# Turning the context, the raw tokens and the spatial weights in small pieces between the first weight chunks of a two-block transformer kernel

## What is computed

```python
def first_block(x, norm1_g, w_in, v_norm_g, w_s, b_s, ...):
    h = rmsnorm(x, norm1_g[l])
    proj = h @ w_in[l]
    u, v_a, q, k, v_b = jnp.split(proj, splits, axis=-1)
    y_a = chunked_spatial_gating(u, v_a, v_norm_g[l], w_s[l], b_s[l])
    q = rmsnorm(q.reshape(bsz, s, B_HEADS, 2, B_HEAD_DIM), q_norm_g[l]).transpose(0, 2, 3, 1, 4)
    k = rmsnorm(k.reshape(bsz, s, B_HEADS, 2, B_HEAD_DIM), k_norm_g[l]).transpose(0, 2, 3, 1, 4)
    ...
    o = diff_attention(q, k, vb, lam, slopes)
    ...
    x = x + merged @ w_out[l]
    x = x + hierarchical_moe(...)

def second_block(x, c, ctx, c_ctx, ada_w, ...):
    mx = jnp.split(jax.nn.silu(c) @ ada_w[layer] + ada_b[layer], N_MOD, axis=-1)
    x = x + 0.5 * mx[2][:, None] * swiglu(modulate(rms_norm(x), mx[0], mx[1]), ...)
    ctx = ctx + 0.5 * mc[2][:, None] * swiglu(modulate(rms_norm(ctx), mc[0], mc[1]), ...)
    ...
```

## Time and profile before

| | us |
|---|---|
| median of three runs | 2301.84 (2301.64 to 2302.30) |
| profiled execution, span | 2299.9 |
| PE busy | 2229.5 (97% of the span) |
| DVE busy | 1352.3 (59%) |
| ACT busy | 699.8 (30%) |
| chain that ended last, share on PE | 88% |

### The profile page before, as it was taken

The page is one execution under the profiler, slowest core; times in us unless marked ns, Lnnn a source line. Parts: engine busy times, 40 slices in busy tenths (PEclk is TensorE's granted clock), DMA queues, the critical chain, the costliest instruction groups (busy, mean ns, idle before and its releaser), DMA issues.

```text
span 2299.9 us, 32019 instructions
## 1 busy us (share of the span) xinstructions
PE 2229.5 (97%) x13550; PEld 1821.4 (79%) x13550; DVE 1352.3 (59%) x1893; ACT 699.8 (30%) x967; POOL 208.4 (9%) x241
## 2 busy tenths in 40 slices
PE   7988989999999999999999999999999999999998
PEld 6878984455488888889679888888888888968998
DVE  5786554333387657652558755745756663656554
ACT  6444421111142112223543212213222212454333
POOL 2001100000011000130021000012000002002000
PEclk9999999999999999999999999999999999999999
DMA  9623757999866556432114645634646543405573
GB/s 297 220 92 118 258 199 317 420 421 421 357 191 173 172 164 194 140 111 74 38 37 138 178 142 156 186 91 117 193 119 191 163 143 107 128 20 140 165 203 117
DMA packets 378189, 408.86 MB, mean 178 GB/s; under 512 B 11754, under 2 KB 343007, under 8 KB 362303
## 3 DMA queue, kind: packets, MB, share of 16 engines
q1 hardware_dynamic: 355886, 325.55, 43.1%
q0 software_dynamic: 21568, 80.14, 11.2%
q10 hardware_dynamic: 592, 1.12, 0.1%
HBM read 405.71 MB, written 1.05 MB: 177 GB/s over the span
## 4 chain that ended last, share of the span: by engine, by line
PE 88%; DVE 7%; ACT 3%; issue 1%; DMA 1%; SPq 0%; DVEq 0%; ACTq 0%
PE B L1828 23%; PE B L1830 23%; PE B L1829 23%; PE B L2240 6%; PE B L2260 3%; PE B L2192 2%; DVE LO L692 2%; PE B L2180 1%; ACT HI L1391 1%; PE B L2570 1%; DVE HF L1050 1%; PE B L1961 1%; PE B L2544 1%; DMA XS<-in_ctx 1%; PE B L2554 1%
## 5 line engine op out<-in xcount | busy, mean ns | idle before, releaser
L1828 PE MATMUL B<-hH,HI 128*128 128x512 f32 (+1 forms) x1936 | 664.4, 343 | 12.4 <-DVE hL L1038 6.5
L1829 PE MATMUL B<-hL,HI 128*128 128x512 f32 (+1 forms) x1936 | 654.7, 338 | 0.0
L1830 PE MATMUL B<-hH,LO 128*128 128x512 f32 (+1 forms) x1936 | 654.5, 338 | 0.0
L692 DVE TENSOR_TENSOR LO<-RAW,HI 128x2048 fp32r<-128x2048 f32 (+3 forms) x218 | 443.8, 2038 | 117.6 <-ACT HI L1391 111.9
L1391 ACT ACTIVATE HI<-RAW 128x2048 fp32r<-128x2048 f32 (+3 forms) x218 | 368.6, 1692 | 345.8 <-PE B L1830 285.6
L1828 PEld LDWEIGHTS B<-hH,HI 128*128 128x128 f32 x1936 | 369.6, 191 | 62.2 <-issue 12.1
L1830 PEld LDWEIGHTS B<-hH,LO 128*128 128x128 f32 x1936 | 369.5, 191 | 39.8
L1829 PEld LDWEIGHTS B<-hL,HI 128*128 128x128 f32 x1936 | 369.8, 191 | 38.5 <-issue 1.2
L778 DVE SCALAR_TENSOR_TENSOR MACC<-MADW,CS,MACC 128x1024 f32<-128x1024 f32 x224 | 277.5, 1280 | 10.0 <-DMA MADW<-in_ada_w 4.3
L1828 PE MATMUL B<-aH,HI 128*128 128x512 f32 (+1 forms) x770 | 269.5, 350 | 0.0
L1830 PE MATMUL B<-aH,LO 128*128 128x512 f32 (+1 forms) x770 | 269.1, 349 | 0.0
(11 more groups left out here) (381 smaller groups left out, 2628.7 us busy)
## 6 DMA issues: line engine op xcount, KB each, us to landing
RAW<-in_ffn_w_gu SPq DMA_DIRECT2D x176, 512.0 KB, 5.2
W<-in_w SPq DMA_DIRECT2D x78, 1024.0 KB, 11.9
MADW<-in_ada_w POOLq DMA_DIRECT2D x128, 512.0 KB, 3.9
W2T<-in_w SPq DMA_DIRECT2D x39, 1024.0 KB, 12.1
RAW<-in_w_in SPq DMA_DIRECT2D x60, 512.0 KB, 4.8
RAW<-in_ffn_w_down SPq DMA_DIRECT2D x56, 384.0 KB, 3.6
RAW<-in_ffn_w_down SPq DMA_DIRECT2D x56, 320.0 KB, 4.2
RAW<-in_w_out SPq DMA_DIRECT2D x24, 512.0 KB, 4.4
```

Of the source, the lines that this page charges most:

```text
L692: V.tensor_tensor(LO[s][:, :words], RAW[s][:, :words], HI[t.hi[s]][:, :words].bitcast(F32), ALU.subtract).then_inc(lo_done[s], 1)
L1828: mm(o, wh, xh, start=first, stop=False, **more)
L1829: mm(o, wh, xl, start=False, stop=False, **more)
L1830: return mm(o, wl, xh, start=False, stop=last, **more)
```

## The change

PE's block behind chunk 0 is now only the three parameter transposes (`parameters`). The 32 transposes of context and raw tokens are eight units, and two of them (8 transposes) follow the matmuls of each of the chunks c = 1 to 4 (`TURN_CHUNKS`), ahead of that chunk's `stats`. The 8 transposes of the spatial weights (`spatial_weights`) follow those of chunk 5. The banks 6, 7 and 1 are now taken in turn over all eight units. On ACT, the two copies of each pair of units stand behind the `root` of the same chunk, and Silu and the `WST` copies behind the `root` of chunk 5. DVE, POOL and SP have the same instructions in the same order. POOL's wait for the turned spatial weights is released from chunk 5 in place of chunk 0.

On ACT:

```diff
+        TURN_CHUNKS = range(1, 5)
...
-            def to_features():
-                for v in (1, 0):
-                    for c in range(4):
-                        got("x_done")
-                        A.activation(XC[:, 2 * c:2 * c + 2, v * S:(v + 1) * S], bank2(X_BANKS[c % 3]), ACT.Copy)\
-                            .then_inc(E["x_copied"], 1)
+            def to_features(u):
+
+                v, c = 1 - u // 4, u % 4
+                got("x_done")
+                A.activation(XC[:, 2 * c:2 * c + 2, v * S:(v + 1) * S], bank2(X_BANKS[u % 3]), ACT.Copy)\
+                    .then_inc(E["x_copied"], 1)
...
             def other_inputs():
 
-                to_features()
                 got("params_ready")
...
             for c in range(12):
                 prep()
-                if c == 0:
-                    other_inputs()
                 products()
...
                     root(B[2 + (c - 1) % 2][:], R[(c - 1) % 2][:])
+                if c in TURN_CHUNKS:
+                    for i in range(2):
+                        to_features(2 * (c - TURN_CHUNKS[0]) + i)
+                elif c == TURN_CHUNKS[-1] + 1:
+                    other_inputs()
```

On PE:

```diff
                 used(ins, s)
                 if c == 0:
-                    other_inputs()
+                    parameters()
                     pe.wait_ge(E["mats_loaded"], 16)
+                elif c in TURN_CHUNKS:
+                    for i in range(2):
+                        to_features(2 * (c - TURN_CHUNKS[0]) + i)
+                elif c == TURN_CHUNKS[-1] + 1:
+                    spatial_weights()
                 if 1 <= c <= 8:
                     stats(MEAN_HD, c - 1, 2 + (c - 1) % 2)
```

More of the change, by code:

```diff
@@ L1900, in _, with parameters @@
                 ins.then_inc(E["xn_done"], 1)
-            def other_inputs():
+            def parameters():
                 pe.wait_ge(E["rows_loaded"], dma_total["rows"])
@@ L1909, in other_inputs, with to_features, spatial_weights @@
                 ins.then_inc(E["params_done"], 1)
[L1910 to L1919, removed]
+            def to_features(u):
+                v, c = 1 - u // 4, u % 4
+                if u == 0:
+                    pe.wait_ge(E["ctx_loaded"], 16)
+                b = X_BANKS[u % 3]
+                claim(b, "x_copied")
+                for m in range(2):
+                    for blk in range(TB):
+                        ins = nc.tensor.transpose(bank2(b)[:, m, blk * P:(blk + 1) * P],
+                                                  XS[:, v, blk, (2 * c + m) * P:(2 * c + m + 1) * P], mat(IDENT))
+                ins.then_inc(E["x_done"], 1)
+            def spatial_weights():
                 pe.wait_ge(E["ws_masked"], 1)
```

## The result

| | before | after |
|---|---|---|
| median, 10 runs each | 2304.94 us (2300.98 to 2306.88) | 2309.45 us (2307.92 to 2311.76) |
| ratio to before, 95% interval | | 1.0022 (1.0013 to 1.0031) |
| profiled execution, span | 2299.9 us | 2308.0 us |
| mean granted clock of that execution | 0.991 | 0.987 |

The change makes the kernel slower by 0.22%, which is 5.1 us by the ratio, with an interval of 3.0 to 7.1; the two medians are 4.5 us apart. The three runs of before that the prediction had were all near its fast end; with ten runs its median is 3.1 us higher.

A forecast was written before the change was run, and what follows sets the result against it. PE, busy for 97% of the span, was taken as the bound. Waits +2.0 and clock +2.0 made 4.0 us: 2299.9 + 4.0 = 2303.9 of span, with 1.9 around it 2305.8 us; range 2302.9 to 2308.2.

The forecast's parts named there:

- The base: Starting time of the forecast: profiled span 2299.9 us, with 1.9 between that span and the median, before adding 4.0 us.
- Chunk 1: PE's start of chunk 1, released by LO: at 26.68 in place of 29.31, after standing still for 3.92 us.
- The transposes: Behind chunks 1 to 4: eight cost PE 0.91 us, unhidden at full time; no wait ahead of chunks 3 to 6.
- Chunk 7: Ahead of chunk 7: PE waits 1.13 us for LO, behind ACT's root, table load, Silu and WST copies.
- The waits: PE's changed waits and moved work up to chunk 8's end, 84.55 against 82.56 before: a cost of 2.0 us.
- The clock: Behind the new 3.92 us wait PE's clock falls for a stretch of 4 us, costing half of it, 2.0 us.
- low clock for longer: Rival at chunk 1 and part of chunk 2: over 5.2 us of PE work low, loss over 4.6 in all; chance 0.32.
- The drain: Rival at ACT's table switches: load plus a drain of about 1380 ns, +5.4 us in all, 2307.2; chance 0.03.

## Why the prediction was wrong

Its 2305.8 us and its range to 2308.2 missed the 2309.45 that was measured. The change it forecast, 4.0 us slower, lies inside the measured 3.0 to 7.1. Point by point:

**The base was drawn from the fast end.** This is the step that failed: "2299.9 + 4.0 = 2303.9 of span; with the 1.9 around it ... 2305.8". The three runs of before agreed within 0.7 us, and I took them for the kernel. Ten runs have it at 2304.94; the medians beside the three sets of experiments were 2305.87, 2304.55 and 2303.65. In the first of these sets, the 11 runs of before with a granted clock of 0.99 and over took 2300.5 to 2304.4 us, the 20 with 0.987 or 0.988 took 2304.6 to 2308.3. The profile of before had 0.991, that of the changed kernel 0.987. In the second set the two groups overlap (2300.3 to 2305.5 and 2304.6 to 2308.8), so the clock is not all of it. The forecast of a difference was added to a time 3.1 us too low, of the 3.6 us by which the result was missed, and the range had nothing for that. All three among the fastest four of ten is 1 in 30 by chance; the three sets ran on three chips, and whether the first three runs were lucky or taken where the level is lower stays open. The other 0.5 us, or 1.1 by the ratio, is the difference itself. The forecast gave 0.60 to one under 4.6 us and 0.38 to a slower one; 4.5 by the medians and 5.1 by the ratio lie on either side.

**Where the clock falls elsewhere differs from one execution to the next.** I read in the earlier trace rows that it stays at 2.4 GHz through about 2.7 us without work. In the changed kernel's profile it fell at that very place:

```profile
305.67 0.39 PE L1831 MATMUL B<-MH,HI 128*128 128x256 f32 x1 [2.70 <-DVE ML L699]
```

```profile
307.20:310.40 3.20, 3.20 (x17) 3.20 (x16) 1.82 (x1) 0.00 (x0) 0.00 (x0) 0.50 0.93 328
652.00:655.20 3.20, 3.20 (x17) 3.20 (x17) 1.19 (x4) 0.00 (x0) 0.00 (x0) 0.50 0.00 0
```

The first window is the fall behind this wait; the second is another at 652 us, where before has full clock. The wait is 2.70 us in both kernels, which are the same from there on, and the second profile of the changed kernel has full clock there again:

```profile
299.00:312.00 13.00, 10.30 (x90) 10.11 (x90) 8.90 (x9) 3.83 (x2) 0.00 (x0) 1.00 0.73 243
```

One row of one execution, which I used as "stays", was one of two outcomes. This wait, 2.69 or 2.70 us, is in all twelve profiles: in five the clock fell behind it and in seven it did not. DVE's rows, counted from the statistics behind chunk 8, show what a fall costs: against before, those five lose 1.6 us at this place and the other six less than 0.1.

The same rows account for the 4.3 us by which the first profile of the changed kernel is longer behind chunk 8. Up to 190 us they are in step with before's within 0.05 us. Then it loses 2.6 near 200, where two stretches are low (3.4 us from 198 and 6.8 from 208) and before has one of 3.4, then 1.6 at the wait above and 1.5 at 652, and gains 1.2 near 2100, where before is low for longer; the rest is 0.2 or less each, and 0.3 at the end. The second profile loses 3.0 near 200, gains the same 1.2 and is 1.6 longer. The place near 200, before and in the first profile of the changed kernel:

```profile
191.00:205.90 14.90, 12.61 (x102) 11.85 (x102) 8.15 (x11) 11.27 (x14) 0.00 (x0) 1.00 0.50 163
205.95:209.37 3.42, 3.42 (x19) 3.42 (x18) 2.29 (x1) 2.12 (x2) 0.00 (x0) 0.50 0.02 6
```

```profile
197.90:201.30 3.40, 3.28 (x16) 2.98 (x16) 2.75 (x4) 2.32 (x5) 0.00 (x0) 0.50 0.74 257
208.10:214.90 6.80, 6.80 (x34) 6.80 (x34) 2.50 (x2) 3.45 (x4) 0.00 (x0) 0.50 0.35 122
```

**Chunk 1** came as worked out: LO at 24.74 for 24.33 (chunk 0 ended 0.4 later), a wait of 4.00 for 3.92.

**The transposes** cost 0.87 us for eight (34.50 to 35.37), for 0.91, and are not hidden. The steps from chunk to chunk are 7.48 to 7.49 (35.37, 42.86), for 7.52. There is no wait ahead of chunks 3 to 6. The statistics behind chunk 8 were forecast near 86.5 and start at 86.36; that is partly luck, since a start 0.4 later and a clock cost 0.5 smaller than forecast cancel.

**Chunk 7** had an idle row of 0.94 us for 1.13, made by ACT's work as described; the run with the early Silu took it away.

**The waits** were sized at 2.0 us. The run with PE kept at work has 62.06 less 60.16, 1.9.

**The clock** was sized at 2.0 us. It was 1.5 in the first profile. In the second the stretch is 0.85 longer at the same waits, which makes 2.3, and with the early Silu the clock was low from inside the wait to 31.6. The 2.0 is between them, but two things in it were off. A matmul takes 0.213 us at 1.2 GHz and 0.12 at 2.4, so 16 of them lose 1.5 us and 25 lose 2.3: that is 44% of the low time and not half. And the second profile has 5.3 us of work at low clock, at the border of the rival "low clock for longer" (more than 5.2); the one with the early Silu has 5.1, the first 3.3. The trace also bears out the rule of the Trainium skill (TensorE: Matmul & The Clock Gate, HAM oscillation) that was set beside it, for this place and in all four profiles that kept a long wait there (4.0, 4.0, 4.0 and 5.8 us), and in none of the other eight.

**The drain** behind a table load did not show: 67.15 + 1.28 = 68.43, and Silu starts at 68.44. That rival is out; the drain of 1380 ns in the Trainium skill (ScalarE: Activation LUTs, What ACT_TABLE_LOAD costs) has no counterpart here.

**What I did not see** were two things in the rows that I had. I read the wait of 0.81 us as "until ACT has emptied banks", without asking why the banks were short, and so took the new turn of banks for a detail. And I held that POOL's loads did not matter; in the changed kernel they did not, because the third and fourth were held back to chunk 5, but they bind as soon as PE gets ahead.

**Open.** Most of the cost is shown in the stretch (3.4 us in one profile, 4.2 in the other, against 5.1 and 5.3 by the ratios). The 1.1 to 1.7 us that remain are inside the intervals, and no run tells whether they are chance or belong to the change. The place near 200 us is where to look: against before's one profile the others stand there between 1.5 us less and 3.1 more, kernels with and without the change among them, and both profiles of the changed kernel are near the upper end.

## What to carry to other kernels

Before work is taken out of a place where an engine waits, find the wait that stands behind it: here DVE's unpacking and splitting kept chunk 1 until 4 us behind chunk 0, and the transposes had been filling that time for nothing. Moving them into stretches without a gap made each cost its full time, left the gap empty, and let the clock fall. What paid was the opposite, to fit the work to the gap: start with the data that is there, keep the turn of banks, copy at once, and hold back the transfers that nobody needs yet. These were tried as a bundle; of its parts only the turn of banks ran alone, and the held loads as an addition. And where single runs of a kernel have levels a few microseconds apart, three that agree are no median.

## What the hardware showed that I had not expected

The program alone does not settle the granted clock. The same wait of 2.70 us was followed by full clock in seven profiles and by some 3.4 us at half in five, and the two profiles of the changed kernel are one of each; the same 4.00 us wait cost 1.5 in one and 2.3 us in another. The runs of one kernel spread over some 8 us (2300.34 to 2308.84 for before); in the profiles that were laid side by side, the differences stand where the clock differs. The other surprise is small: beside POOL's masking of the spatial weights, the two engines' rows depended on who had started first. Where DVE's LO began first (25.40), POOL's mask was stretched to 3.00 us; where POOL's began first (25.14 against 25.43), it took 1.09 and the LO 2.95 in place of 2.28. Over the twelve profiles, LO began first in eleven, and in all of them the mask ended 0.95 to 1.06 us behind LO's end, however early it had begun; that is about the 1.09 us that it takes by itself. So POOL's mask makes next to no headway while LO runs. That POOL's in turn held up the later LO rests on one profile.

```profile
25.64 3.00 POOL L633 TENSOR_SCALAR_AFFINE_SELECT WS<-WS 128x1024 f32<-128x1024 f32 x1 [11.75 <-DMA WS<-in_w_s]
```

```profile
25.14 1.09 POOL L633 TENSOR_SCALAR_AFFINE_SELECT WS<-WS 128x1024 f32<-128x1024 f32 x1 [11.30 <-DMA WS<-in_w_s]
```

The first row is POOL's in the kernel with 31 filling matmuls, the second in the one that has the early Silu besides.
